# The chunk loop of a state-space mixer, reordered inside a fused two-block kernel

## The reference

```python
xdt = x * dt[..., None]
a = dt * a_head                                  # per chunk and head
a_cs = cumsum(a)                                 # inside a chunk
cb = einsum('bclgn,bcsgn->bgcls', cm, bm)
y_diag = einsum(cb * exp(segsum(a)), xdt)        # inside a chunk
decay_states = exp(a_cs[..., -1:] - a_cs)
states = einsum(bm, decay_states, xdt)           # what a chunk adds to the state
# the state runs from chunk to chunk: S = S * exp(total of a) + states
y_off = einsum(cm, S before the chunk, exp(a_cs))
y = y_diag + y_off + x * d_skip
y = rmsnorm(y * silu(z)) 
```

## Time and profile before

| what | us |
|---|---|
| median of three runs | 4126.79 |
| lowest and highest run | 4124.66, 4131.62 |
| the profiled execution: span from first to last instruction | 4130.0 |
| TensorE busy in it | 3731.3 |
| VectorE, ScalarE, GpSimd busy | 2244.4, 1520.3, 1130.7 |
| the loop over the chunks | 160.46 |

### The profile page before, as it was taken

How to read it: one execution, slowest core, us unless ns; L and a number is a source line. 1 busy time by engine, 2 the same in 40 slices (tenths; PEclk the granted TensorE clock), 3 DMA queues, 4 the chain that set the end, 5 groups by cost and what they waited for, 6 DMA issues and landing times. The chain is left out here.

```text
span 4130.0 us, 44122 instructions
## 1 busy us (share of the span) xinstructions
PE 3731.3 (90%) x16834; PEld 2944.3 (71%) x16834; DVE 2244.4 (54%) x2559; ACT 1520.3 (37%) x1906; POOL 1130.7 (27%) x593
## 2 busy tenths in 40 slices
PE   4899987677799999978888899999979899999997
PEld 1678876555678778766665657777767688888886
DVE  6468547665688888866634132222236453354338
ACT  3221211143677777734220222222232332332234
POOL 2322212034211111133321211222134344444443
PEclk8899998778899999969987999999989999999999
DMA  4411123655899999944321211211154323323233
GB/s 154 119 47 69 65 87 120 203 181 189 310 400 398 400 400 399 397 183 145 140 87 41 105 55 52 71 60 63 41 196 141 128 97 97 97 92 97 97 110 125
DMA packets 166353, 646.10 MB, mean 156 GB/s; under 512 B 21112, under 2 KB 46552, under 8 KB 150064
## 3 DMA queue, kind: packets, MB, share of 16 engines
q1 hardware_dynamic: 135424, 555.34, 37.4%
q10 hardware_dynamic: 20400, 56.63, 3.5%
q0 software_dynamic: 10368, 31.91, 2.0%
HBM read 536.52 MB, written 107.30 MB: 156 GB/s over the span
## 5 line engine op out<-in xcount | busy, mean ns | idle before, releaser
L3553 POOL TENSOR_TENSOR t_wl<-t_raw,t_wh 128x1024 fp32r<-128x1024 f32 x160 | 386.6, 2417 | 521.2 <-ACT t_wh L3599 521.2
L99 PE MATMUL m_b<-b_high,m_high 128*128 128x512 f32 x960 | 417.4, 435 | 10.5 <-POOL m_low L2442 7.9
L100 PE MATMUL m_b<-b_rest,m_high 128*128 128x512 f32 x960 | 392.9, 409 | 0.0
L101 PE MATMUL m_b<-b_high,m_low 128*128 128x512 f32 x960 | 384.2, 400 | 0.0
L2440 POOL TENSOR_TENSOR m_high<-m_raw,m_one 128x1024 fp32r<-128x1024 f32 x60 | 119.2, 1986 | 857.5 <-PE m_b L101 792.4
L99 PE MATMUL t_b<-b_high,t_wh 128*128 128x512 f32 x768 | 302.3, 394 | 16.4 <-POOL t_wl L3553 16.4
L100 PE MATMUL t_b<-b_rest,t_wh 128*128 128x512 f32 x768 | 299.9, 391 | 0.0
L101 PE MATMUL t_b<-b_high,t_wl 128*128 128x512 f32 x768 | 299.8, 390 | 0.0
L3599 ACT ACTIVATE t_wh<-t_raw 128x1024 fp32r<-128x1024 f32 x160 | 169.1, 1057 | 311.8 <-PE t_b L101 298.3
L99 PE MATMUL zs_z<-zs_hs,zs_high 128*128 128x512 f32 (+1 forms) x584 | 225.8, 387 | 27.7 <-POOL zs_hs L278 27.7
L99 PEld LDWEIGHTS m_b<-b_high,m_high 128*128 128x128 f32 x960 | 187.3, 195 | 75.1 <-issue 16.2
(11 more groups left out here) (651 smaller groups left out, 8869.1 us busy)
## 6 DMA issues: line engine op xcount, KB each, us to landing
moe_raw<-in_expert_w SPq DMA_DIRECT2D x79, 2048.0 KB, 10.1
ex_raw<-in_expert_w SPq DMA_DIRECT2D x39, 2048.0 KB, 10.6
t_raw<-in_w_ff SPq DMA_DIRECT2D x128, 512.0 KB, 3.4
m_raw<-in_w_ug SPq DMA_DIRECT2D x60, 512.0 KB, 4.4
yrows<-ex_y ACTq DMA_DIRECT2D x38, 512.0 KB, 11.2
zs_raw<-in_ada_w SPq DMA_DIRECT2D x32, 512.0 KB, 3.9
gates<-m_ob SPq DMA_DIRECT2D x32, 512.0 KB, 2.9
me_g<-gates SPq DMA_DIRECT2D x32, 512.0 KB, 3.7
```

The source lines that it names most:

```text
L99: nc.tensor.matmul(out, w[0], x[0], start=first, stop=False)
L100: nc.tensor.matmul(out, w[0], x[1], start=False, stop=False)
L101: return nc.tensor.matmul(out, w[1], x[0], start=False, stop=last)
L3553: self.nc.gpsimd.tensor_tensor(self.wl[u % self.NW][:], self.raw[u % 2][:], self.wh[u % self.NW][:].bitcast(F32), ALU.subtract).then_inc(s ...
```

## The change

In `StateSpace`:

- TensorE: `rows(i + 1)` is issued directly behind the state products of chunk i. The projection unit of a chunk is cut in two halves, one ahead of the diagonal products and one behind them. The diagonal products read `xt`. The state products of chunk i also wait for `y_full`, the addition of the diagonal products of chunk i - 1.
- VectorE: ahead of the loop, for each chunk as it is copied, `y` is set to x times d, and `xt` is multiplied by dt in place. `xdt` and the loop's operation for `t` are gone; `xb` has two buffers and is made for chunk i + 1 behind the masks of chunk i. The state's contribution goes through `t` and is added to `y`. The addition of the diagonal products signals `y_full`.
- ScalarE: the drain of a unit comes one chunk later in its program, the last one behind the loop.
- `Projection.settle` turns counted half units into whole ones; `Attention` calls it too, with no difference in what it does.

```diff
@@ -2473,6 +2473,10 @@
             self.unit(pe, self.made + x // 2, part=x % 2)
             self.parts += 1
 
+    def settle(self):
+
+        self.made, self.parts = self.made + self.parts // 2, 0
+
     def take(self, act, count=1):
         for m in range(self.moved, min(self.moved + count, self.total)):
             n, c = divmod(m, 2)
@@ -2740,13 +2744,13 @@
             self.dtr, self.x = f.sb("dtr", [SH, SEQ]), [f.sb(f"x{j}", [P, 3 + SEQ]) for j in range(6)]
         with Stage(nc, q.name + "b") as f:
             self.L, self.M = [f.sb(f"L{j}", [P, SH, P]) for j in range(2)], f.sb("M", [P, SH, P])
-            self.xdt, self.xb, self.S, self.t = (f.sb(n, [P, SH * SHD]) for n in ("xdt", "xb", "S", "t"))
+            self.xb, self.S, self.t = [f.sb(f"xb{j}", [P, SH * SHD]) for j in range(2)], f.sb("S", [P, SH * SHD]), f.sb("t", [P, SH * SHD])
             self.z = f.sb("z", [P, 4, SEQ])
...
 
     def load(self, sp, n):
         if n == U_XBC:
@@ -2802,27 +2806,34 @@
             st.then(V.tensor_tensor(self.L[i % 2][:, 4:8], self.ps[1][:].rearrange("p (h t) -> p h t", h=4), self.acs[:, i, 4:8].unsqueeze(2).broadcast_to([P, 4, P]), ALU.subtract))
             V.tensor_tensor(self.L[i % 2][:], self.L[i % 2][:], C["cut"][:, 0:1, :].broadcast_to([P, SH, P]), ALU.min).then_inc(self.lready, 1)
 
+        def weigh_inputs(i):
+            V.tensor_tensor(heads(self.xb[i % 2][:]), heads(self.xt[:, i]), wide(self.back[:, i]), ALU.mult).then_inc(self.xb_done, 1)
+
+        st.then(V.memset(self.S[:], 0.0))
+        for i in range(NCK):
+            dve.wait_ge(self.moved, i + 1)
+            st.then(V.tensor_tensor(heads(self.y[:, i]), heads(self.xt[:, i]), wide(self.d8[:]), ALU.mult))
+            st.then(V.tensor_tensor(heads(self.xt[:, i]), heads(self.xt[:, i]), wide(self.dt[:, i]), ALU.mult))
         dve.wait_ge(self.exped, 6)
-        dve.wait_ge(self.moved, NCK)
-        st.then(V.memset(self.S[:], 0.0))
+        weigh_inputs(0)
         differences(0)
         for i in range(NCK):
-            st.then(V.tensor_tensor(heads(self.xdt[:]), heads(self.xt[:, i]), wide(self.dt[:, i]), ALU.mult))
-            V.tensor_tensor(heads(self.xb[:]), heads(self.xdt[:]), wide(self.back[:, i]), ALU.mult).then_inc(self.xb_done, 1)
-            st.then(V.tensor_tensor(heads(self.t[:]), heads(self.xt[:, i]), wide(self.d8[:]), ALU.mult))
             dve.wait_ge(self.lexped, i + 1)
             for g in range(2):
                 V.tensor_tensor(self.M[:, 4 * g:4 * g + 4, :], self.L[i % 2][:, 4 * g:4 * g + 4, :],
                                 self.ps[2][:, g * P:(g + 1) * P].unsqueeze(1).broadcast_to([P, 4, P]), ALU.mult).then_inc(self.masked, 1)
+            if i + 1 < NCK:
+                weigh_inputs(i + 1)
             dve.wait_ge(self.summed, 1 + 3 * i + 2)
-            st.then(V.tensor_tensor(heads(self.y[:, i]), heads(self.ps[3][:]), wide(self.eacs[:, i]), ALU.mult))
+            st.then(V.tensor_tensor(heads(self.t[:]), heads(self.ps[3][:]), wide(self.eacs[:, i]), ALU.mult))
             st.then(V.tensor_tensor(self.y[:, i], self.y[:, i], self.t[:], ALU.add))
             st.then(V.tensor_tensor(heads(self.S[:]), heads(self.S[:]), wide(self.tot[:, i]), ALU.mult))
             V.tensor_tensor(self.S[:], self.S[:], self.ps[4][:], ALU.add).then_inc(self.y_done, 1)
             if i + 1 < NCK:
                 differences(i + 1)
             dve.wait_ge(self.summed, 1 + 3 * i + 3)
-            st.then(V.tensor_tensor(self.y[:, i], self.y[:, i], self.ps[3][:], ALU.add))
+            V.tensor_tensor(self.y[:, i], self.y[:, i], self.ps[3][:], ALU.add).then_inc(self.y_full, 1)
+        dve.wait_ge(self.y_full, NCK)
         for i in range(NCK):
             dve.wait_ge(self.z_turned, i + 1)
             V.tensor_tensor(self.y[:, i], self.y[:, i], self.ps[i % 2][:], ALU.mult).then_inc(self.gated, 1)
@@ -2871,20 +2882,23 @@
         rows(0)
         for i in range(NCK):
             pe.wait_ge(self.y_done, i)
+            pe.wait_ge(self.y_full, i)
             pe.wait_ge(self.xb_done, i + 1)
             r = [slice(0, 64), slice(64, P)]
             mm_(ps[3][:, 0:256], self.xo[r[0], 5, i * P:(i + 1) * P], self.S[r[0], 0:256], start=True, stop=True).then_inc(self.begun, 1)
-            mm_(ps[4][:], self.bt[:, i], self.xb[:], start=True, stop=True).then_inc(self.summed, 1)
+            mm_(ps[4][:], self.bt[:, i], self.xb[i % 2][:], start=True, stop=True).then_inc(self.summed, 1)
             pe.wait_ge(self.begun, i + 1)
             mm_(ps[3][:, 256:512], self.xo[r[1], 5, i * P:(i + 1) * P], self.S[r[1], 256:512], start=True, stop=True).then_inc(self.summed, 1)
-            self.F.multiply(pe, 1)
             pe.wait_ge(self.masked, 2 * i + 2)
             if i + 1 < NCK:
                 rows(i + 1)
+            self.F.halves(pe, 1)
             pe.wait_ge(self.y_done, i + 1)
             for h in range(SH):
-                mm = mm_(ps[3][:, h * SHD:(h + 1) * SHD], self.M[:, h, :], self.xdt[:, h * SHD:(h + 1) * SHD], start=True, stop=True)
+                mm = mm_(ps[3][:, h * SHD:(h + 1) * SHD], self.M[:, h, :], self.xt[:, i, h * SHD:(h + 1) * SHD], start=True, stop=True)
             mm.then_inc(self.summed, 1)
+            self.F.halves(pe, 1)
+        self.F.settle()
         self.F.multiply(pe, 1)
         pe.wait_ge(self.z_silu, 4)
         for i in range(NCK):
@@ -2932,7 +2946,9 @@
         for i in range(NCK):
             act.wait_ge(self.lready, i + 1)
             S.activation(self.L[i % 2][:], self.L[i % 2][:], ACT.Exp).then_inc(self.lexped, 1)
-            self.F.take(act, 1)
+            if i:
+                self.F.take(act, 1)
+        self.F.take(act, 1)
         act.wait_ge(self.z_in, 64)
         for n in range(4):
             S.activation(self.z[:, n, :], self.z[:, n, :], ACT.Silu).then_inc(self.z_silu, 1)
@@ -3086,7 +3102,7 @@
                 if h + 1 < MH:
                     ready(h + 1)
                     score(n + 1)
-        F.made += F.parts // 2
+        F.settle()
 
     def scalar(self, act):
         S, ps, F = self.nc.scalar, self.ps, self.F
```

More of the change, by code:

```diff
@@ L2746, in __init__ @@
          self.rowed, self.lready, self.lexped, self.masked, self.xb_done, self.y_done, self.z_silu, self.z_turned, self.gated, self.squared, self.rooted,
-         self.scaled, self.o_turned, self.o_moved, self.stored, self.first, self.begun) = (s.sem("s_" + n) for n in (
+         self.scaled, self.o_turned, self.o_moved, self.stored, self.first, self.begun, self.y_full) = (s.sem("s_" + n) for n in (
              "got", "x_in", "dt_in", "z_in", "own", "convd", "silu", "turned", "moved", "d_turned", "ready", "exped", "summed", "rowed", "lready", "lexped",
-             "masked", "xb_done", "y_done", "z_silu", "z_turned", "gated", "squared", "rooted", "scaled", "o_turned", "o_moved", "stored", "first", "begun"))
+             "masked", "xb_done", "y_done", "z_silu", "z_turned", "gated", "squared", "rooted", "scaled", "o_turned", "o_moved", "stored", "first", "begun", "y_full"))
     def load(self, sp, n):
```

## The result

| what | before | after |
|---|---|---|
| median of the runs (4 each), us | 4128.59 | 4069.22 |
| lowest and highest run | 4124.66, 4131.62 | 4064.64, 4073.41 |
| span of the profiled execution | 4130.0 | 4066.5 |
| the loop over the chunks | 160.46 | 103.73 |

The ratio is 0.9854, with a 95% interval from 0.9843 to 0.9866: 59 us less. My estimate was 4075, 52 us less, with a range from 4066 to 4096.

The account below looks back on a forecast made before the run. TensorE was taken to bound the loop, through 3.0 us waits for VectorE and the half clock behind them. The 160.46 us stretch becomes 108.1, gain 52.4, less 0.5 behind the loop, 51.9: median 4075 us, range 4066 to 4096.

Parts of the forecast that it names:

- What bounds the loop: Chunk loop: TensorE waits 3.0 us for VectorE each chunk, and each wait halves its clock for some 10 us.
- The three waits of a steady chunk: TensorE's waits for VectorE in the loop: all met, y_done 2.7 us early, y_full 2.1, masks 3.0.
- A steady chunk: TensorE at full clock: state products 2.3, rows 2.9, unit 5.6, diagonals 2.0, together 12.8 us.
- 108.1: Loop stretch of 160.46 us after the change: 99.9 of work, new waits 0.7 + 2.8 + 0.3, cold stretch 4.4.
- Chunk 0: First chunk: TensorE waits 0.7 us for xb(0) and 2.8 for masks(0), then one half-clock stretch costing 4.4.
- GpSimd ... No cost: GpSimd in the loop: halves a weight tile in 4.25 us, has 25.6 for two chunks, so no cost.
- Behind the loop: After the loop: silu of z, about 5.9 us on ScalarE against one unit of 5.6, idles TensorE 0.5.
- the stages behind unchanged in length: Stages after the loop: a sign of being right was that their length stays unchanged.
- The clock in part of every chunk: Rival, loop: each chunk keeps a cold stretch of the present size, gain 21.6 - 0.5, 4106 us; chance 0.11.
- A wait in place of the old one: Rival, loop: the masks(0) wait repeats each chunk, period again 20.2 us, no change, 4127; chance 0.04.
- Slower: Rival, loop: clock never returns to 1.00, a chunk takes 24.2 us, 27 longer in all, 4154; chance 0.03.
- The rule of the Trainium skill: Rule against the change: short pauses between matmul groups make the clock alternate; the time would be the first rival's.

Follow-up runs that it names:

- The experiment with the whole unit: Changed kernel with the projection unit whole ahead of the diagonal products, no second half behind them; 4078.06 us, ratio 0.9879.
- TensorE's part alone: Kernel before with TensorE's and ScalarE's new order and the signal y_full, VectorE's old order kept; 4067.96 us, ratio 0.9856.
- differences first: Changed kernel with the differences of chunk 0 ahead of its xb; 4067.21 us, ratio 0.9845.
- rows ahead without VectorE's part: Kernel before with TensorE's and ScalarE's new order, plus first decay rows between halves of the last unit ahead of the loop; 4070.20 us, ratio 0.9858.
- block version: Changed kernel with state products, rows and diagonal products in one block, whole projection unit behind them; 4086.95 us, ratio 0.9906.

## Why the estimate held, step by step

**What bounds the loop** was read rightly: TensorE's wait of 3.0 for VectorE and the half clock behind it. Both are gone from the steady chunks.

**The three waits of a steady chunk** are met, each with a little less than the margin of the sum: y_done 2.3 us early instead of 2.7, y_full 2.0 instead of 2.1, the masks 2.5 instead of 3.0. The experiment with the whole unit shows what covers y_full: without the second half it is a wait of 0.8.

**A steady chunk** was 12.8 in the sum and is 12.25. I had put the diagonals at 2.0, from the start of the first to the end of the last; the next matmul doesn't wait for that end, and from start to start they are 1.72. State products and rows are 1.68 + 3.01 = 4.69 instead of 5.2; 0.22 of that is the last state product beside the first of the rows, and the rest is not traced to a term. Against that, the two halves take 2.90 + 2.94 = 5.84 where I had 5.6 and the cut at nothing, with up to 0.4 a chunk only in the range. Together this is 0.55 less. Over seven chunks it is 3.9 of the 4.4 us by which the loop came out below 108.1.

**Chunk 0** lost what I had counted, but by another way, and that the totals agree is luck. I had 0.7 for xb(0) and 2.8 for the masks, together 3.5; it was 2.4 and 0.75, together 3.1. The step that failed is "GpSimd ... No cost": its subtraction held VectorE's xb(0) up by 1.75 us. The half clock came as counted, 4.4 in the sum, and 17.79 - 12.25 - 0.75 = 4.8 measured; only it began behind the first wait, not the second. Other orders show that this price doesn't follow the length of the wait: chunk 0 was 2.3 us longer than a steady chunk behind a wait of 4.5 (TensorE's part alone), 3.2 behind 3.5 (differences first), 4.7 behind 2.9 (rows ahead without VectorE's part). In three steady chunks the same subtraction stretched VectorE's addition to y (L2829) from 0.69 to 1.97; that is 1.3 of the 2.3 us by which y_done was early, so it cost nothing here, and 1.3 us a time in the block version.

**Behind the loop** I had 0.5 for the silu of z; TensorE waited 0.3. I had "the stages behind unchanged in length", and that was wrong by some us: 5.2 us less in the first profile, 1.8 less in the second, nearly all of it in parts where the granted clock differs. It makes the difference between my 52 and the 59 together with the 4.4 of the loop.

**The rivals.** The clock in part of every chunk: no, 1.00 in all steady chunks, and in five of six in the block version's profile. A wait in place of the old one: not in the changed kernel; where the second half is taken away there is one, of 0.8. Slower: no. (Its 10.2 for a unit at half clock is not twice 5.6, as its words say; twice would be 11.2 and the time 4162. The 10.2 fits the trace of before, where a projection matmul starts every 0.43 us at that clock.) The rule of the Trainium skill on pauses that make the clock alternate ("TensorE: Matmul & The Clock Gate", "A second HAM failure mode: psum-queue depth-cycling") is not put to the test by the changed kernel's turns, which have no pause: TensorE is busy for all of the 12.25 us. Nor do the 37 small instructions of the earlier trace rows speak against it, as the prediction has it, since TensorE is busy for 4.81 of their 4.82 us. The experiments bear on it: with waits of 0.8 a chunk the clock fell in one chunk of six, and with 1.5 it was lowered in all, which is in its direction.

What stays open is why one wait lowers the clock and another of like length doesn't. 0.8 mostly did not, 1.5 did in all six chunks, 1.84 in the block version did once in three times, 3.0 always did in the loop of before, and 2.9 behind the loop left it at 1.00 in the changed kernel's first profile. So the length of a wait alone doesn't settle it. The spread of 20 us in the runs of the block version is open too.

## What to carry to other kernels

Put an engine's filler work behind the step that feeds the other engine, not ahead of it, and keep some of it for the next hand-over: the order state products, rows, half the filler, diagonals, the other half gave the whole gain, with the filler whole ahead of the diagonals it was 51 us of it, and reordering the engine that was late gave 27. Price each wait of TensorE with the clock that it can cost: in the old loop 3.0 us of wait cost 4.4 us more, in every chunk; elsewhere a wait of that length cost nothing. When a chunk loop is steady, read its first turn by itself; here all the waits that were left in the loop lay there, and moving one step ahead of the loop won 4 to 8 us more.

## What the hardware showed

- A VectorE operation of 128x512 with both inputs in SBUF that starts while a GpSimd tensor operation runs does not run beside it here: wherever in GpSimd's operation it started, it ended 0.5 to 0.6 us behind the end of that one (2.44 instead of 0.69 for xb(0), 1.97 for L2829, 2.27 and 2.83 without VectorE's part), for L2440 and L2442 alike. With one input in PSUM it took 0.69, in the middle of GpSimd's operation as well. The Trainium skill, "GPSIMD Engine Reference", section "1. Specifications", says that GpSimd shares its SBUF interfaces with VectorE and names operations with two SBUF inputs as a case of contention; the trace agrees, and here it is a wait for the end of the running operation, not a slower pace.
- Two products in different halves of the array, 64 partitions each, ran side by side in a plain sequence, with no more done for it than the order of the instructions: 0.22 us a chunk.
- Behind one and the same wait of 3 us, the same twenty passes took 9.36, 10.93 and 12.27 us, at a mean granted clock of 1.00, 0.84 and 0.75. The first two are of the same kernel, and the stretch around them differed by 3.4 us between its two profiles. So a difference of 2 or 3 us between kernels with such waits behind the change can't be put down to the change by the times alone.
- A wait of 1.84 us at the same place of the same loop left the clock at 1.00 twice and was followed by 0.50 the third time.
